# Eight steps of the first group's experts to a block of the second group's pass, in place of twelve

## What is computed

```python
xn = rmsnorm(x, g_mix)
xr, yr, ca, cb, ga, gb = split(xn @ w_in)
branch_a = (h * gelu(yr)) @ w_a
branch_b = silu(layernorm(dc)) @ w_b
merged = sigmoid(ga) * branch_a + sigmoid(gb) * branch_b
x = x + merged @ w_out
# experts, for blocks of 128 tokens
q = xb @ w_q
s1, s2 = scores of q against keys1, keys2          # 8 heads x 128 keys each
e, g = 16 best of the sums of the 16 best of each, softmax of them
act = gelu(einsum('thkd,td->thk', u_tab[e], xb))
out = einsum('thk,thkd->td', g * act, v_tab[e])
```

## Time and profile before

| | us |
|---|---|
| median of three runs | 4137.86 (4135.47 to 4138.53) |
| profiled execution, device time | 4142.44 |
| its span, first to last instruction | 4140.7 |
| PE, DVE, POOL, ACT busy | 3160.5, 2436.7, 1543.4, 557.3 |
| moved by DMA | 1372.28 MB, 331 GB/s over the span |

### The profile page before, as it was taken

One profiled execution on the slowest core, in us unless ns is written; L12 is line 12 of the kernel. 1 busy time (PEld: TensorE's weight loads), 2 busy tenths in 40 slices (PEclk: granted clock), 3 DMA queues, 4 the chain that ended last, 5 costly groups with the idle time before them and its releaser, 6 DMA issues.

```text
span 4140.7 us, 36271 instructions
## 1 busy us (share of the span) xinstructions
PE 3160.5 (76%) x11848; PEld 1897.9 (46%) x11848; DVE 2436.7 (59%) x3355; ACT 557.3 (13%) x1118; POOL 1543.4 (37%) x1154
## 2 busy tenths in 40 slices
PE   6999899879788866839802777777777777777778
PEld 5999889875445433525500222222222222222233
DVE  2788810146787784775667556655655665566540
ACT  4444310110010000001101001001001100110010
POOL 2000000014454543552335545554454554444432
PEclk9999999889999988979956999999999999999999
DMA  4322367579999998996978999999999999999997
GB/s 124 86 84 84 118 211 242 179 276 335 391 379 389 392 381 312 368 376 224 348 264 346 412 421 421 421 419 422 418 419 418 417 419 416 422 412 422 421 396 253
DMA packets 406310, 1372.28 MB, mean 331 GB/s; under 512 B 24449, under 2 KB 264065, under 8 KB 264735
## 3 DMA queue, kind: packets, MB, share of 16 engines
q0 software_dynamic: 157584, 1145.05, 68.3%
q1 hardware_dynamic: 246382, 221.85, 16.9%
q10 hardware_dynamic: 2257, 4.40, 0.3%
HBM read 1363.20 MB, written 8.86 MB: 331 GB/s over the span
## 4 chain that ended last, share of the span: by engine, by line
DMA 47%; PE 31%; DVE 12%; issue 7%; POOL 2%; ACT 1%; SPq 0%; POOLq 0%; DVEq 0%; ACTq 0%
DMA region<-in_v_tab_dram,region 35%; PE ps L1359 11%; DMA region<-in_u_tab_dram,region 10%; PE ps L1542 8%; DVE region L1183 3%; PE ps L1342 3%; PE ps L1344 3%; PE ps L1343 3%; DVE region L1236 2%; POOL region L523 2%; DVE region L1174 1%; DMA region<-in_state_rnn_h_dram 1%; DMA region<-in_w_q_dram 1%; DVE region L1135 0%; DVE region L1025 0%
## 5 line engine op out<-in xcount | busy, mean ns | idle before, releaser
L1542 PE MATMUL ps<-region,region 128*128 128x512 f32 x3072 | 1418.3, 607 | 579.2 <-DMA region<-in_v_tab_dram,region 572.9
L1359 PE MATMUL ps<-region,region 128*128 128x160 f32 (+1 forms) x5120 | 1241.3, 405 | 182.7 <-DVE region L1071 60.7
L1236 DVE SCALAR_TENSOR_TENSOR region<-region,region 128x2048 f32<-128x2048 f32 x384 | 874.2, 2291 | 624.7 <-DMA region<-in_u_tab_dram,region 624.7
L1542 PEld LDWEIGHTS ps<-region,region 128*128 128x128 f32 x3072 | 561.2, 191 | 1436.4 <-issue 1140.7
L523 POOL DMA_INDIRECT region<-in_v_tab_dram,region x544 | 744.5, 1369 | 1143.5 <-PE ps L1542 554.8
L1359 PEld LDWEIGHTS ps<-region,region 128*128 128x128 f32 x5120 | 863.9, 197 | 552.4 <-issue 114.3
L523 POOL DMA_INDIRECT region<-in_u_tab_dram,region x544 | 756.2, 1390 | 952.9 <-DVE region L1164 340.7
L1183 DVE SCALAR_TENSOR_TENSOR region<-region,region,region 128x2048 f32<-128x2048 f32 x160 | 376.1, 2351 | 245.1 <-DMA region<-in_v_tab_dram,region 245.1
L1174 DVE SCALAR_TENSOR_TENSOR region<-region,region 128x2048 f32<-128x2048 f32 x160 | 365.2, 2285 | 22.3 <-DMA region<-in_u_tab_dram,region 22.3
L1342 PE MATMUL ps<-region,region 128*128 128x272 f32 x1024 | 297.4, 290 | 0.0
L1344 PE MATMUL ps<-region,region 128*128 128x272 f32 x1024 | 296.4, 289 | 0.0
(11 more groups left out here) (202 smaller groups left out, 1432.9 us busy)
## 6 DMA issues: line engine op xcount, KB each, us to landing
region<-in_w_in_dram SPq DMA_DIRECT2D x192, 512.0 KB
region<-in_w_out_dram SPq DMA_DIRECT2D x64, 512.0 KB
region<-in_w_q_dram SPq DMA_DIRECT2D x64, 512.0 KB
region<-in_w_a_dram SPq DMA_DIRECT2D x32, 512.0 KB
region<-in_w_b_dram SPq DMA_DIRECT2D x32, 512.0 KB
region<-in_u_tab_dram,region POOLq DMA_INDIRECT x544, 11.6
region<-in_v_tab_dram,region POOLq DMA_INDIRECT x544, 15.3
region<-in_x_prompt_dram SPq DMA_DIRECT2D x7, 1024.0 KB, 15.3
```

The costliest lines, as they stand in the source:

```text
L1236: stt(out=u_b[s], in0=u_b[s], scalar=1.0, in1=xn_tile(UNITS_A + u), op0=ALU.mult, op1=ALU.mult, accum_out=dots[u % 2][:, k:k + 1]).then_in ...
L1359: last = mm(outs[n][:, 0:WIDTH[g]], wide[s][:, q, n * P:(n + 1) * P], rhs(k), start=(k == 0), stop=(k == n_k - 1))
L1542: last = mm(acc[n][:, b * 512:(b + 1) * 512], diag[:, k, :], v_b[s][:, b * 512:(b + 1) * 512], start=(k == 0), stop=(k == TOPK - 1))
```

## The change

Three functions that deal the steps out are changed; DVE and ACT both call them, in their programs' same places.

```diff
 def steps_branch(m):
-    return 14 + 12 * m, 26 + 12 * m
+    return 14 + 8 * m, 22 + 8 * m
 
 
 def steps_out(j):
-    return 110 + 2 * j, 112 + 2 * j
+    first = 78 + 3 * (j // 2) + j % 2
+    return first, first + 1 + j % 2
 
 
 def steps_query(h):
-    return 142 + 4 * h, 146 + 4 * h
+    return 102 + 3 * h, 105 + 3 * h
```

## The result

| | before | changed |
|---|---|---|
| median, us | 4138.19 (4135.47 to 4142.28, 4 runs) | 4273.67 (4267.82 to 4285.79, 4 runs) |
| ratio to before | | 1.033, 95% interval 1.0306 to 1.0355 |
| profiled execution, its span | 4142.44, 4140.7 | 4271.12, 4269.3 |

The change costs 135 us by the medians and 129 us by the two profiled spans; the forecast was 74, in a range of 12 to 137. It has the forecast's sign and lies at the upper edge of its range, 2 us inside it.

The account below looks back on a forecast made before the run. The prediction took transfers, not PE, to pace the branch pass. Its three terms, -121 - 33 + 228, summed to +74 us, 4212 us on a median of 4137.9, with a range of 4150 to 4275 (+12 to +137).

Parts of the forecast that it names:

- Term 1: Branch pass, 670.6 us before: blocks of 8 steps at 68 us, PE the bound, 549 us in all, so -121.
- "4" for weights: Branch pass: PE was to lose 4 us a block waiting for weights while gathers run, added to 62.4.
- I leave 1.6: Branch pass: 1.6 us a block allowed for PE's slower clock after a wait, added to 62.4.
- rival 1: Branch pass and steps behind w_q, with w_out: PE and the tail both at their floors, net -12 us; chance 0.06.
- Term 2: w_out, 263 us before: 8 steps less, but steps catch up with PE; 230 us, so -33, between -20 and -45.
- Term 3: w_q to the last value row's end, 253.6 us before: 481.5 us, so +228, between +200 and +258.
- The stall: Start of w_q: DVE waits for ACT's gelu behind head 3 and scores behind head 4; route ends at 151.5 us.
- I take 5.2 us a step: Behind w_q: 44.5 steps with dots at 5.2 us, 231 us, brought to 250 with x1, g_final and routes.
- Last phase: From the fold to the end, the second group's 24 units: same length as before, 2015 us.
- The signs: Changed profile: blocks 66 to 70 us, DMA under 350 GB/s, last score about 1900, fold about 2200, value rows 5 to 5.5.
- Rival 2: From 937 to 2125: DMA a shared stock, 417 MB conserved at 351 GB/s, end moves under 8 us; chance 0.05.
- Rival 3: Worse ACT coupling or weight starvation: branch blocks 74 us, tail 6.2 us a step, +165 us in all; chance 0.06.

## Why the prediction was right in its sign and short in its size

- **What bounds each stretch.** Right. The DMA paced the blocks at 12 steps (but for the first, where its share was 0.93) and PE at 8; blocks are 70.8 us apart (1081.12 to 1222.68 holds two), waits on merges are gone, and at 10 and 8 steps the gain bends as it must.
- **Term 1, -121.** Measured -105. Both additions to 62.4 were too small. "4" for weights: the waits took 43.5 / 8 = 5.4 us a block, 11 us in all; this is the larger part. "I leave 1.6" for the slower clock: PE's matmuls took 518.7 / 8 = 64.8 us, 2.4 over 62.4, at a granted clock of 0.96; that is 6 us. DVE's wait for scores in every second block came as told, four times, to 31.5 us. The ends -147 and -163 (rival 1) should read -146 and -162 by their own figures.
- **Term 2, -33.** Measured -36, with some luck. As named, the steps catch up with PE, and the route of step 99 stands on DVE's path between the last sums. But DVE did not wait for its staging: ACT staged the scores at 1677.17, 177 us in and not 186, and DVE came to them at 1688.90. From 1676.73 to the last sum at 1711.94 DVE worked almost without a gap, 35 us where the forecast had 27.5. The two errors nearly cancel. PE's wait of 19.05 us at 1697.00 is real but cost nothing here, since DVE was not waiting for PE then.
- **Term 3, +228.** Measured +271, beyond its upper end of +258. It is made of three parts. The stall: the route ended 162.4 us into w_q and not 151.5, because PE's products of heads 1 and 2, with steps 102 to 112 beside them, starved for weights (9.5 us of waits in w_q). The steps with dots: from 1890.47 to some 2170, 280 us and not 250. "I take 5.2 us a step" is the term that was mis-sized. The step took 6.0 us on the mean, by a round trip through two buffers in which the issue is 2.24 us beside a dot and not the 0.94 of the earlier trace rows, and the landing 6.7 us and not 4.5. That gives 44.5 x 6.05 = 269 us; the other 11 lie with the routes and the 5 MB of x1 and g_final, which no run parted. The value 280 stood in the forecast as the upper end, from the pace beside weights, and was the better row; that it is met exactly is chance, since it leaves the routes out. The rows without dots: 82 for 80.
- **The range.** The terms missed by +17, -3 and +43 us. Term 3 lay outside its own range, and the whole stayed inside by 2 us only because the other two did not come near their upper ends.
- **Last phase.** Right: 2016.5 us for 2015.4.
- **The signs.** DMA under 350 GB/s in the branch pass and the unchanged last phase held. Blocks (70.8 us for 66 to 70), last score (1924 for 1900), fold (2253 for 2200) and value rows (6.0 for 5 to 5.5) all came out late.
- **Rivals.** Rival 1 (a tail at DVE's 4.48) falls: even with three buffers six steps behind a route reach that pace, and then it is 4.97. Rival 2 (conserved transfers) falls: the pass up to the fold moved the same bytes at 316 GB/s (934.75 to 2252.78) and not 351. Rival 3's tail at 6.2 a step was near (286 us for 280), its branch pass at 74 us was not; its total of +165 is 30 us off the measured 135, the forecast's +74 is 61.
- Taking the stall of step 113 for a fixed price was also too simple. It could be moved, and it came back at the next gelu; set well, it was worth 32 us in w_q and behind it, of which 13 (spans) to 25 (ratios) showed in the whole.

## What to carry over

Before work is moved from a stretch with one bound to an empty one, work out the pace of the empty stretch as a cycle: buffer freed, issue, landing, use, divided by the number of buffers. Here it was 6.05 us, above both DVE's 4.48 and the 4.97 that the DMA needs for two tiles at 422 GB/s, so the naked steps cost more than the 5.4 that covered ones cost. And an engine's waits at the start of a stage are the place to move work *to*: steps put there gained 1%.

## What the hardware showed that was not expected

- POOL's issue of a gather is not one length. It took 0.93 to 0.95 us when it began outside DVE's dots and value rows (40 issues from 1890 to 2255), and 1.9 to 3.1 us when it began during one (65 of 66; one that began 0.08 us into a row took 0.94). In the changed kernel:

```profile
2104.31 1.97 POOL L524 DMA_INDIRECT region<-in_u_tab_dram,region  x1 [0.30 <-issue]
...
2108.78 2.98 POOL L524 DMA_INDIRECT region<-in_u_tab_dram,region  x1 [0.30 <-issue]
...
2114.26 0.93 POOL L524 DMA_INDIRECT region<-in_u_tab_dram,region  x1 [0.30 <-issue]
```

DVE's rows in the same time, by their starts, are 2103.12 (value), 2105.38 (dot), 2108.59 (value), 2110.86 (dot, to 2113.15) and, after a wait, 2114.36. The first issue ends at 2106.28 and the second at 2111.76, each 0.8 us behind the end of the row it began in; the third began in the wait. All 65 end 0.80 to 0.82 us behind their row. It is as if the issue stood until the row was over. The Trainium skill (GPSIMD Engine Reference, Specifications) has this engine's SBUF interface shared with VectorE, with contention from DVE instructions with two SBUF inputs; the trace agrees as far as it goes, since both rows read two tiles in SBUF, and gives the price here, 1 to 2 us an issue. That the interface is the cause is not shown: no run put a DVE instruction with one input in their place.
- One queue of gathers alone reached 422 GB/s over 50 us in the kernel with three buffers. The 358 of the Trainium skill (DMA: Bandwidth & Descriptors, Where 436 GB/s comes from), which the forecast weighed and set aside, is there half of what one HBM stack gives its two cores; for this kernel on one core it was no limit.
